# Seven block products for the up products of two MLPs, taken in turns with down tiles of half depth

## The reference, cut to what matters

```python
def mlp(h, w_up, w_down):
    return jnp.square(jax.nn.relu(h @ w_up)) @ w_down
...
        xp = xp + yp
        xs = xs + ys
        xp = xp + mlp(rmsnorm(xp, norm_mlp_g[layer]), w_up[layer], w_down[layer])
        xs = xs + mlp(rmsnorm(xs, norm_mlp_g[layer]), w_up[layer], w_down[layer])
```

## Time and profile before

| | |
|---|---|
| median of 3 runs | 1794.64 us (1790.83 to 1795.55) |
| profiled execution, span | 1793.1 us |
| PE busy | 1736.8 us (97%) |
| PE weight loads busy | 1623.3 us (91%) |
| DVE busy | 954.7 us (53%) |
| ACT busy | 548.6 us (31%) |
| POOL busy | 159.4 us (9%) |

### The profile page before, as it was taken

The page is one execution under the profiler, slowest core; times in us unless marked ns, Lnnn a source line. Parts: engine busy times, 40 slices in busy tenths (PEclk is TensorE's granted clock), DMA queues, the critical chain, the costliest instruction groups (busy, mean ns, idle before and its releaser), DMA issues.

```text
span 1793.1 us, 36785 instructions
## 1 busy us (share of the span) xinstructions
PE 1736.8 (97%) x15035; PEld 1623.3 (91%) x15035; DVE 954.7 (53%) x1454; ACT 548.6 (31%) x1075; POOL 159.4 (9%) x212
## 2 busy tenths in 40 slices
PE   7998999999999999999999999999999999999998
PEld 6995667899999999999898898878799999999998
DVE  4336776655353433444587774677665435343454
ACT  4114556432121222231511413443133212122222
POOL 0710000320000000020000000012012000000002
PEclk9999999999999999999999999999999999999999
DMA  8219999337676767544368678523033767422221
GB/s 277 71 50 363 351 353 346 124 118 257 234 257 234 257 233 257 187 131 158 96 198 284 211 253 274 197 83 102 33 121 120 278 227 260 173 79 88 75 91 55
DMA packets 167162, 338.82 MB, mean 189 GB/s; under 512 B 9178, under 2 KB 116500, under 8 KB 165437
## 3 DMA queue, kind: packets, MB, share of 16 engines
q1 hardware_dynamic: 164691, 249.74, 41.3%
q0 software_dynamic: 2240, 87.41, 13.0%
q10 hardware_dynamic: 114, 0.03, 0.0%
HBM read 324.36 MB, written 100.19 MB: 237 GB/s over the span
## 4 chain that ended last, share of the span: by engine, by line
PE 86%; DVE 7%; ACT 2%; DMA 2%; issue 1%; SPq 1%; ACTq 0%; DVEq 0%
PE pp L667 55%; PE pp L977 16%; PE pp L727 2%; PE pp L926 1%; DMA kvring<-in_cache_b_kv 1%; PE pp L741 1%; PE pp L761 1%; PE pp L1084 1%; PE pp L1131 1%; PE pp L1180 1%; PE pp L1109 1%; DVE stat L1668 1%; DVE pp L1666 1%; ACT e_p L2163 1%; DMA vring<-in_cache_d_kv 1%
## 5 line engine op out<-in xcount | busy, mean ns | idle before, releaser
L1943 ACT ACTIVATE whi<-raw 128x1024 fp32r<-128x1024 f32 x208 | 220.6, 1060 | 899.7 <-PE pp L667 687.7
L667 PE MATMUL pp<-a_hi,whi 128*128 128x288 f32 x1280 | 275.8, 297 | 1.0 <-DVE zbuf L1335 0.7
L667 PE MATMUL pp<-a_lo,whi 128*128 128x288 f32 x1280 | 274.6, 296 | 0.0
L667 PE MATMUL pp<-a_hi,wlo 128*128 128x288 f32 x1280 | 274.4, 296 | 0.0
L1292 DVE TENSOR_TENSOR wlo<-raw,whi 128x1024 fp32r<-128x1024 f32 x208 | 256.0, 1231 | 30.5 <-ACT whi L1943 30.4
L667 PE MATMUL pp<-b_hi,whi 128*128 128x288 f32 x1152 | 247.0, 296 | 0.0
L667 PE MATMUL pp<-b_lo,whi 128*128 128x288 f32 x1152 | 247.0, 296 | 0.0
L667 PE MATMUL pp<-b_hi,wlo 128*128 128x288 f32 x1152 | 246.9, 296 | 0.0
L1351 DVE TENSOR_TENSOR x<-x,pp 128x576 f32 (+1 forms) x80 | 60.4, 755 | 295.1 <-PE pp L667 284.0
L667 PEld LDWEIGHTS pp<-a_hi,whi 128*128 128x128 f32 x1280 | 206.6, 189 | 2.3 <-issue 1.7
L667 PEld LDWEIGHTS pp<-a_lo,whi 128*128 128x128 f32 x1280 | 206.7, 189 | 0.0
(11 more groups left out here) (304 smaller groups left out, 2062.9 us busy)
## 6 DMA issues: line engine op xcount, KB each, us to landing
kvring<-in_cache_b_kv SPq DMA_DIRECT2D x128, 512.0 KB, 5.6
out_new_d_sample<-in_cache_d_kv POOLq DMA_DIRECT2D x32, 2040.0 KB, 8.5
raw<-in_w_up SPq DMA_DIRECT2D x32, 1024.0 KB, 5.4
raw<-in_w_down SPq DMA_DIRECT2D x32, 1024.0 KB, 5.2
kring<-in_cache_d_kv SPq DMA_DIRECT2D x104, 256.0 KB, 3.3
vring<-in_cache_d_kv SPq DMA_DIRECT2D x104, 256.0 KB, 5.3
raw<-in_w_in_cd SPq DMA_DIRECT2D x24, 1024.0 KB, 5.2
out_new_d_sample<-in_cache_d_kv POOLq DMA_DIRECT2D x8, 2016.0 KB, 8.3
```

Of the source, the lines that this page charges most:

```text
L667: last = pe.matmul(acc_h[s][:, h, :], w[s][:, k, :], m[:, k, NH * h:NH * h + NH], start=(at_ == 0 and n == 0), stop=(at_ == KT_N - 1 and n ...
L1943: act.activation(whi_v[j], raw_v[q // 2][:, :, j, :], ACT.Copy).then_inc(whi_ready, 1)
```

## The change

The up products of a pair of hidden tiles are made as Strassen and Winograd do it, with seven block products in place of eight. The operands are cut in blocks: a pair of k tiles (j = 0, 1) against a pair of hidden tiles (e = 0, 1) for the weights, and the same pair of k tiles against the two halves of the columns for the input. The weight blocks are a11 = (e0, j0), a12 = (e1, j0), a21 = (e0, j1), a22 = (e1, j1); DVE makes four sums of them, S0 = a21 + a22, S1 = S0 - a11, S2 = a11 - a21 and S3 = a12 - S1. Of the input, DVE makes four differences of blocks per pair of k tiles while the stage ahead of the MLP ends (form_differences), and ACT and DVE write their high and low parts, t_hi and t_lo. A product has 4 pairs of k tiles x 3 (high and low) = 12 matmuls of 128x288, which all add into one PSUM bank; further products add into banks 4 and 5 on top of an earlier one, after ACT has copied that one's state out. DVE adds the copies and the banks up to the two tiles of the pair.

An MLP now makes its first 4 up tiles as before. Then come 14 rounds of 7 products (two hidden tiles) and 4 down tiles of half depth (4 hidden tiles in place of 8, so 24 matmuls, and half of x's 8 tiles a round), and at the end 8 more down tiles of half depth. The rounds run as the first, a loop of three times four, and the last; before, each chunk was a step of a loop whose inner loops had four tiles.

ACT now takes the relu, out of PSUM for the first tiles, and a separate square; DVE multiplies the square by r squared, for which the reciprocal of the mean square stays without a root (L1966 isn't executed in the MLPs). Weights are split in blocks of 512 columns and each raw buffer has a fixed use: raw[0] has the up weights of a round, raw[1] those of its four down tiles. SP issues them in turns, the up load when five of the seven parts of the round before are split (form_lo), the down load when all four parts of it are (wlo_ready). The first load of the stage after the first MLP goes ahead of its last down load. Some semaphores are merged. POOL's copies wait for the same counts of tile_done; an MLP counts 68 tiles in place of 64.

```diff
-T_CD = T_M0 + 64
+ROUNDS, MLP_T = 14, 68
+T_CD = T_M0 + MLP_T
...
+PRODUCTS = ((None, 0), (2, 5), (1, 4), (None, 2), (0, 1), (None, 6), (3, 3))
...
+        def rounds(engine, body):
+            body(0, 0)
+            with engine.Fori(0, 3) as i:
+                for r0 in range(1, 5):
+                    body(i, r0)
+            body(3, 1)
...
+                    sp.dma_start(raw_v[0].rearrange("p k j n -> p k (j n)"),
+                                 up.rearrange("(k p) n -> p k n", p=P)[:, :, ds(r * 256 + 512, 256)]
+                                 ).then_inc(raw_loaded[0], 16)
...
+                def down_four(c, h):
+                    sp.wait_ge(wlo_ready, c * 8 + (t0 + 4 + 4 * h))
+                    sp.dma_start(raw_d, down[ds(c, 1), :, 512 * h:512 * h + 512].rearrange("o (k p) n -> p (o k) n", p=P)
+                                 ).then_inc(raw_loaded[1], 16)
...
-                G0, fa, fb = t0 // 4, 8 * (1 + 2 * L), (8, 48)[L]
-                dense(lambda i: i + G0, 2, ahk, alk, a_ready, fa, hook=mean_square(1 + 2 * L), peel=True)
-                dense(lambda i: i + (G0 + 2), 2, bhk, blk, b_ready, fb)
...
+                def product(i, r0, m):
+                    f, s_ = PRODUCTS[m][1], U_SLOT[m]
+                    pe.wait_ge(form_lo, times(i, r0, 7) + (forms + MADE[m] + 1))
...
+                    for kk in range(4):
+                        for n, (w, hi) in enumerate(((u_hi, True), (u_hi, False), (u_lo, True))):
+                            last = pe.matmul(U_BANK[m], w[s_][:, kk, :], operand(f, kk, hi),
+                                             start=(kk == 0 and n == 0 and m in (0, 1, 3)), stop=(kk == 3 and n == 2),
+                                             skip_group_check=(m in (2, 4, 5, 6)))
+                    last.then_inc(u_done, 1)
+                def down_tile(i, r0, n):
...
+                    pe.wait_ge(wlo_ready, times(i, r0, 4) + (t0 + 4 + n + 1))
+                    pe.wait_ge(acc_free, times(i, r0, 4) + (t0 + 4 + n + 1))
+                    w_hi, w_lo = down_hi(times(i, r0, 1), n), down_lo(times(i, r0, 1), n)
+                    for k in range(4):
+                        if r0 % 2 == 0 and n == 0 and k in (0, 2):
+                            pe.wait_ge(b_ready, c4 + (B_TILES[L] + 2 + k))
+                        for m, (w, b) in enumerate(((w_hi, b_hi_), (w_hi, b_lo_), (w_lo, b_hi_))):
+                            for h in range(2):
+                                last = pe.matmul(acc_h[s_][:, h, :], w[:, k, :], b[:, k0 + k, NH * h:NH * h + NH],
+                                                 start=(k == 0 and m == 0), stop=(k == 3 and m == 2))
+                    last.then_inc(tile_done, 1)
+                def one_round(i, r0):
+                    for m, n in ((0, None), (1, 0), (2, None), (3, 1), (4, None), (5, 2), (6, 3)):
+                        product(i, r0, m)
+                        if n is not None:
+                            down_tile(i, r0, n)
...
-                dve.tensor_tensor(z.rearrange("p (h c) -> p h c", h=2), acc_h[j], r_h, ALU.mult).then_inc(acc_free, 1)
...
+                def weight_sum(i, r0, n):
+                    a11, a12, a21, a22 = (raw_u[:, :, 0, 0, :], raw_u[:, :, 1, 0, :], raw_u[:, :, 0, 1, :],
+                                          raw_u[:, :, 1, 1, :])
+                    now = times(i, r0, 4) + made
+                    if n == 2:
+                        dve.wait_ge(form_lo, times(i, r0, 7) + forms)
+                        dve.wait_ge(raw_loaded[0], times(i, r0, 16) + 16 * up_loads(L))
+                        dve.tensor_tensor(w_sum[2], a11, a21, ALU.subtract).then_inc(form_sums, 1)
+                    if n == 0:
+                        dve.tensor_tensor(w_sum[0], a21, a22, ALU.add).then_inc(form_sums, 1)
+                    if n == 1:
+                        dve.wait_ge(form_sums, now + 2)
+                        dve.tensor_tensor(w_sum[1], w_sum[0], a11, ALU.subtract).then_inc(form_sums, 1)
+                    if n == 3:
+                        dve.wait_ge(form_sums, now + 3)
+                        dve.wait_ge(form_lo, times(i, r0, 7) + (forms + 2))
+                        dve.tensor_tensor(w_sum[3], a12, w_sum[1], ALU.subtract).then_inc(form_sums, 1)
+                def rooted(n, j):
+                    dve.wait_ge(u_squared, n + squared)
+                    dve.tensor_tensor(sq_t[j], sq_t[j], rnorm[:, :], ALU.mult).then_inc(sq_up, 1)
...
+                def one_round(i, r0):
+                    more = not (isinstance(i, int) and times(i, r0, 1) == ROUNDS - 1)
+                    pairs = times(i, r0, 2)
+                    b0 = 4 + 2 * r0
+                    form(i, r0, 4)
+                    add_down(i, r0, 0)
+                    add_up(i, r0, 3, 0, 0, 1)
+                    form(i, r0, 6)
+                    add_down(i, r0, 1)
+                    if more:
+                        weight_sum(i, r0 + 1, 2)
+                    form_down(i, r0 + 1, 0)
+                    if more:
+                        form(i, r0 + 1, 0)
+                    add_up(i, r0, 4, 1, 1, 2)
+                    if more:
+                        form(i, r0 + 1, 1)
+                    add_up(i, r0, 5, 1, 0, 3)
+                    if more:
+                        weight_sum(i, r0 + 1, 0)
+                        weight_sum(i, r0 + 1, 1)
+                    add_down(i, r0, 2)
+                    form_down(i, r0 + 1, 1)
+                    if more:
+                        form(i, r0 + 1, 2)
+                    rooted(pairs + 5, 1)
+                    if more:
+                        weight_sum(i, r0 + 1, 3)
+                    rooted(pairs + 6, 0)
+                    if more:
+                        form(i, r0 + 1, 3)
+                    add_down(i, r0, 3)
+                    square_lo(pairs + 5, 1, (b0 + 1) % 8)
+                    square_lo(pairs + 6, 0, b0 % 8)
+                    if more:
+                        form(i, r0 + 1, 5)
+                    form_down(i, r0 + 1, 2)
+                    form_down(i, r0 + 1, 3)
...
+                    act.activation(z_part(0, 0), U_BANK[0], ACT.Copy).then_inc(u_copied, 1)
+                    form(i, r0, 4)
+                    after_up(i, r0, 1)
+                    act.activation(z_part(1, 1), U_BANK[1], ACT.Copy).then_inc(u_copied, 1)
...
+                    act.wait_ge(u_added, times(i, r0, 3) + (added + 3))
+                    act.activation(z_t[1], z_t[1], ACT.Relu).then_inc(u_relu, 1)
...
```

More of the change, by code:

```diff
@@ L47 @@
 T_AB, T_OA, T_M0 = 0, 16, 24
-T_CD = T_M0 + 64
+ROUNDS, MLP_T = 14, 68
+T_CD = T_M0 + MLP_T
 T_OC = T_CD + 48
 T_M1 = T_OC + 8
-T_END = T_M1 + 64
+T_END = T_M1 + MLP_T
+T_MLP = (T_M0, T_M1)
+PRODUCTS = ((None, 0), (2, 5), (1, 4), (None, 2), (0, 1), (None, 6), (3, 3))
+MADE = {m: n for n, m in enumerate((0, 1, 2, 3, 5, 4, 6))}
+U_SLOT = (0, 1, 2, 3, 4, 5, 3)
+FORMS = 4 + 7 * ROUNDS
+SUMS = 20 + 4 * ROUNDS
+B_TILES = (8, 48)
 C = {}
@@ L491, in matrix, with mlp_weights, up_pair @@
                         unit(w, i * 512 + 256 * s, i * 2 + t0 // 2 + s, s)
-            def mlp_weights(L, t0):
-                up, down = a["w_up"][L], a["w_down"][L].rearrange("(c k) n -> c k n", c=4)
-                with sp.Fori(0, 4) as c:
-                    with sp.Fori(0, 2) as i:
-                        for s in range(2):
-                            unit(up, c * 1024 + i * 512 + 256 * s, c * 8 + i * 2 + t0 // 2 + s, s)
-                    with sp.Fori(0, 2) as i:
-                        for s in range(2):
-                            sp.wait_ge(wlo_ready, (c * 8 + i * 2 + (t0 // 2 + 4 + s)) * 2 - 2)
-                            sp.dma_start(raw_v[s].rearrange("p k j n -> p k (j n)"),
-                                         down[ds(c, 1), :, ds(i * 512 + 256 * s, 256)]
-                                         .rearrange("o (k p) n -> p (o k) n", p=P)).then_inc(raw_loaded[s], 16)
+            def mlp_weights(L, t0, before_last=None):
+                up, down = a["w_up"][L], a["w_down"][L].rearrange("(c k) n -> c k n", c=8)
+                rows = raw_d.rearrange("p k n -> p (k n)")
+                def up_pair(r, wait):
+                    if wait:
+                        sp.wait_ge(form_lo, r * 7 + (FORMS * L + 4 - 2))
+                    else:
+                        sp.wait_ge(wlo_ready, t0 + 2)
+                    sp.dma_start(raw_v[0].rearrange("p k j n -> p k (j n)"),
[5 more added lines that the diff above has]
+                                 ).then_inc(raw_loaded[1], 16)
+                unit(up, 0, t0 // 2, 0)
+                unit(up, 256, t0 // 2 + 1, 1)
+                for h in range(2):
+                    up_pair(h, h > 0)
+                    down_four(0, h)
+                with sp.Fori(1, 7) as i:
+                    for h in range(2):
+                        up_pair(i * 2 + h, True)
+                        down_four(i, h)
+                down_four(7, 0)
+                if before_last:
+                    before_last()
```

(31 more changed lines are left out.)

442 lines of the change are left out of this document (324 added, 118 removed).

## The result

The changed kernel takes 1767.76 us, median of 4 executions (1759.39 to 1772.78), against 1792.74 before (1790.53 to 1795.55): a ratio of 0.985, interval 0.9817 to 0.9884. It is faster by 25.0 us, inside the range, and 9 us slower than forecast. Its executions lie 13 us apart where those of before lay 5 apart. The profiled one has a span of 1763.8 us, 29.3 less than before, where the sum said 36.2.

A forecast was written before the change was run, and what follows sets the result against it. PE's matmuls were taken to bound the MLPs. 44.8 + 0.4 - 2 x 2.1 - 2 x 1.0 - 2.8 = 36.2 us off span 1793.1 gives 1756.9, with 1.5 for the median 1758.4 us; range 1750 to 1784.

The forecast's parts named there:

- The removed matmuls: In both MLPs 336 fewer matmuls of 128x288 at 133.4 ns each: 44.8 us gained; a round takes 24.0 us.
- Adding into one bank: A product's 12 matmuls add into one bank: taken as no loss; rival, products slower than down tiles, 4%.
- The work of the rounds: DVE 17.8 us and ACT 12.6 us of each 24.0 us round, hidden behind the matmuls, costed at nothing.
- The margin at p6: A round's seventh product needs DVE's second product addition by 19.2 us; it was put at 16.2, 3 us to spare.
- One price of a rival: DVE and ACT set the pace: operations a third slower lose about 1.2 us a round, 33 us, 1791; chance 6%.
- the two chains of the prediction: Tightest in a round: DVE's addition before the seventh product, 3 us spare; squares before every second round's first down tile, 2.5.
- The edges: Late down weights and squares at each MLP's start, 2.1 us lost, and at its end, 1.0 us.
- The loops: Rival: PE's longer loop body waits for instruction fetches at its jumps back, 4 x 5.0 = 20 us, 1778; chance 6%.
- The weights: Each round's up and down loads land 7 us after issue, up to about 11 costing nothing; rival, late weights, 14%.
- a load issued 2.5 us ahead of such a copy landed in 5.7: Trace row of the kernel before, issued at 404.7; spoke against small load packets waiting behind those of every cache copy.
- The large copies: Second MLP, round 6: a load beside the two larger cache copies lands 16.2 us after issue; 2.8 us lost, once.
- The clock: No term in the sum; a granted clock below 1.00 in an MLP was listed as a sign of being wrong.

The follow-up runs named there:

- paced ones: Changed kernel with a round's cache copies started after its second and third down tiles, the two 1920 KB copies as eight of 480 KB: 1751.58 us, later 1752.83.

## Why the prediction was right, and where it was off

- *The removed matmuls.* Right: a round of 180 matmuls takes 24.0 us, a product of 12 takes 1.60. Adding into one bank cost nothing here.
- *The work of the rounds.* Right. DVE was put at 17.8 us a round and has 16.17, ACT at 12.6 and has 11.37: single durations were met (below), but neighbours overlap by nearly 0.1 us. The margin at p6 was put at 3 and is 3.3: in the undisturbed round above the second addition ends at 603.86 and p6 starts at 607.12 (timelines of DVE and PE, and then the single durations by groups, 584 to 680 us). My 3.4 in the expectations was read a little too high. One price of a rival does not follow: with durations a third longer the two chains of the prediction still keep about 2.0 and 0.7 us, so they do not give its "1.2 us" lost a round, and no run shows that loss.

```profile
603.41 0.45 DVE L1594 TENSOR_TENSOR zbuf<-zbuf,pp 128x288 f32<-128x288 f32 x1
```

```profile
607.12 0.30 PE L809 MATMUL pp<-a_hi,u_hi 128*128 128x288 f32 x1
```

```profile
L1549 DVE TENSOR_TENSOR d_lo<-raw,d_hi 128x512 fp32r<-128x512 f32 x17 | 11.3, 685 | 0.0
L2316 ACT ACTIVATE d_hi<-raw 128x512 fp32r<-128x512 f32 x16 | 9.6, 625 | 14.3 <-PE pp L826 14.3
L1594 DVE TENSOR_TENSOR zbuf<-zbuf,pp 128x288 f32<-128x288 f32 x12 | 5.4, 450 | 10.1 <-PE pp L809 10.1
L2349 ACT ACTIVATE zbuf<-pp 128x288 f32<-128x288 f32 x4 | 1.6, 410 | 17.5 <-PE pp L809 17.5
```

- *The edges.* Right in place but for the last down weights, which nothing waited for: waits of 0.9, 0.6 and 0.6 us per MLP where 1.2, 0.9 and 0.7 plus 0.3 were said. That the loss of 2.9 us comes so near to the 3.1 said is partly luck: the waits are 2.1 of it, and the rest is slower matmuls just after them, for which the sum had no term.
- *The loops.* No gap at a jump back: in the run without copies no two matmuls of the rounds start more than 0.14 us apart away from the edges. The rival falls.
- *The weights.* Here it was off. The 7 us taken for a landing and the 11 of tolerance were met (10.7 gave no wait, 13.4 waits of 0.7 and 2.3). The step that failed is "a load issued 2.5 us ahead of such a copy landed in 5.7", taken as the rule for a load with a copy behind it. That load had met its copy too: half of the copy had started when it landed (kernel before, from the copy's issue to the landing of the load), as beside the load of 7.2 us above.

```profile
q0 software_dynamic: 16, 1.04, 78.8%
```

So it was one outcome of two, and a rare case: before, only this load and the one of 1388.0 (6.0 us) had a copy less than 3.7 us behind them. Now every round with copies has one 3.0 us behind its down load, which stands 1.2 us behind an up load and takes 7.1 us even without copies. So "hidden" was true of some executions only. The Trainium skill's rule of turns by whole packets (DMA: Bandwidth & Descriptors, Queues, rings and completion order) was set against that 5.7 and weighed too little; the run with pieces of 4 KB agrees with it, 9.5 us at most against 13.4.
- *The large copies* were a term of 2.8 us (5.5 less 3 is rather 2.5), mis-sized. The loads beside them landed in 17.0 and 18.3 us where 16.2 was taken, and the term followed the up load, while the chain goes through the down load, issued 1.2 us later and needed earlier:

```profile
1528.53 18.34 DMA raw<-in_w_down
```

The wait was 5.7, and the slow clock behind it brought the gaps to about 8.1.
- *The clock* was no term at all, though the prediction named a clock below 1.00 in an MLP as a sign of being wrong. It came, behind the long waits.

In sum, the forecast allowed 9.0 us of losses. In the profiled execution the gaps between PE's matmuls come to 2 x 2.9 at the edges, about 5 for late loads in the first MLP and about 8 in the second: 19, hence MLPs of 395.9 and 398.8 us where 391 and 394 were said. The span fell by 3 us more than 44.8 + 0.4 - 19 = 26; the stage between the MLPs was 2.3 us shorter in this execution, and between the last down load of the one and the first up load of the other there lay 566 to 571 us in twelve profiles of kernels that have this stage alike, so nothing follows from that. That the median lies inside the forecast's own range (to 1768) was partly luck: the same kernel gave 1772.71 and 1773.86 in later sets, beyond it. What the rounds can give, 1751.5, is shown twice, without copies and with paced ones.

## What to carry to other kernels

When transfers take new places, look at who starts within a few microseconds of whom: a background copy that cost nothing beside one early load can hold up two just-in-time ones, and start it when the loads of the period have landed. A margin is a time at one place of one queue, not the idle time of an engine; adding work there until it shows measures it. Executions that scatter more than before were here the sign of a race between transfers, and a single profile showed only one of its outcomes. One load that came through beside a copy did not show that the next would.

## What the runs showed of the hardware

- A load with 2 KB rows and a copy in 64 KB pieces issued 2.9 to 3.0 us behind it landed in 7.0 to 8.2 us in most rounds and in 10.6 to 13.4 in others; with the copy 1.4 us behind it, in 11.9 to 13.4 in all nine cases of two profiles. Beside a copy in 4 KB pieces it needed 9.5 at most, and 7.1 without copies.
- After PE waited for 2.3 and 5.7 us the granted clock was 0.52 and 0.51, and 13 and 18 matmuls stood 240 ns apart. After waits of 0.6 to 0.9 us in this kernel only the next one or two were late. The length of the wait does not decide alone: in the run with eight more sums the same wait of 2.5 us was followed by twelve slow matmuls in one round and by none in the next, and the wait of 3.3 us in the run with copies after d1 and d2 by one slow matmul in the first MLP and by 22 in the second.
- A copy of 1920 KB in 4 x 8 pieces took 14.4 and 21.9 us, one of 2040 KB in 32 pieces 7.7 to 10.5. The trace shows that the 32 pieces of the former start four at a time, about 2.3 us apart, those of the latter sixteen at a time. Copies of 480 KB in 16 pieces landed in 3.4 us each.
